# Recurrence of a two-block model on one core: v centred while it is turned, and the departing unit's steps moved

## The reference, cut to what matters

```python
def step(state, inp):
    r_t, w_t, k_t, v_t, aa_t, bb_t = inp
    sa = jnp.einsum('bhij,bhj->bhi', state, aa_t)
    state = (state * w_t[:, :, None, :] + sa[..., None] * bb_t[:, :, None, :]
             + v_t[..., None] * k_t[:, :, None, :])
    y = jnp.einsum('bhij,bhj->bhi', state, r_t)
    return state, y
...
mu = jnp.mean(y, axis=-1, keepdims=True)
var = jnp.mean(jnp.square(y - mu), axis=-1, keepdims=True)
yn = (y - mu) * lax.rsqrt(var + GN_EPS)
yn = yn * gn_w + gn_b
bonus = jnp.sum(r_h * k_h * r_k.astype(jnp.float32), axis=-1, keepdims=True) * v_h
out = (yn + bonus) * heads(g)
```

## Time and profile before

| | us |
|---|---|
| runs before the change | 3271.34, 3264.36, 3263.5 |
| median | 3264.36 |
| profiled execution, its own time | 3259.7 |
| its span in the profile | 3257.9 |
| TensorE busy (matmuls) | 3078.1 |
| VectorE busy | 1979.6 |
| ScalarE busy | 1417.1 |
| mean granted TensorE clock | 0.984 of full speed |

### The profile page before, as it was taken

The page is one execution under the profiler, slowest core; times in us unless marked ns, Lnnn a source line. Parts: engine busy times, 40 slices in busy tenths (PEclk is TensorE's granted clock), DMA queues, the critical chain, the costliest instruction groups (busy, mean ns, idle before and its releaser), DMA issues.

```text
span 3257.9 us, 46321 instructions
## 1 busy us (share of the span) xinstructions
PE 3078.1 (94%) x18478; PEld 2345.0 (72%) x18478; DVE 1979.6 (61%) x3370; ACT 1417.1 (43%) x2611; POOL 0.2 (0%) x4
## 2 busy tenths in 40 slices
PE   8988999999999999899999999888899999999888
PEld 7446666688888887778888666666646887787766
DVE  3635667667666656875555476666543666656675
ACT  2313555645333334553334455555412554444343
POOL 0000000000000000000000000000000000000000
PEclk9999999999999999999999899999999999999999
DMA  7510000042333356543333400000043334455545
GB/s 272 194 46 1 1 1 1 13 155 68 94 104 97 104 173 220 178 153 98 118 109 107 164 17 18 22 20 17 19 157 137 126 106 144 142 184 203 185 164 181
DMA packets 254519, 351.27 MB, mean 108 GB/s; under 512 B 12384, under 2 KB 142048, under 8 KB 251104
## 3 DMA queue, kind: packets, MB, share of 16 engines
q1 hardware_dynamic: 254304, 348.30, 32.0%
HBM read 263.84 MB, written 84.41 MB: 107 GB/s over the span
## 4 chain that ended last, share of the span: by engine, by line
PE 73%; DVE 11%; DMA 8%; issue 4%; ACT 3%; SPq 0%; DVEq 0%; ACTq 0%
PE ps L198 71%; DMA wr<-in_w_down 6%; DVE wl L406 3%; DMA hid<-ob 2%; PE ps L1572 1%; DVE NM L2429 1%; PE ps L934 1%; ACT wh L382 1%; PE ps L2868 0%; DMA wr<-hid 0%; DVE MM L3187 0%; DVE ob L1325 0%; DVE Yf L507 0%; DVE QT L2448 0%; DVE RT L2447 0%
## 5 line engine op out<-in xcount | busy, mean ns | idle before, releaser
L198 PE MATMUL ps<-ffn_h,wh 128*128 128x512 f32 x2176 | 672.9, 390 | 12.4 <-DVE ob L1325 9.2
L406 DVE TENSOR_TENSOR wl<-wr,wh 128x512 fp32r<-128x512 f32 x610 | 403.2, 688 | 276.0 <-ACT wh L382 272.5
L382 ACT ACTIVATE wh<-wr 128x512 fp32r<-128x512 f32 x610 | 363.9, 624 | 459.7 <-PE ps L198 280.4
L198 PEld LDWEIGHTS ps<-ffn_h,wh 128*128 128x128 f32 x2176 | 408.0, 188 | 101.7 <-DVE ob L1325 13.5
L198 PE MATMUL ps<-ffn_h,wl 128*128 128x512 f32 x1088 | 423.9, 390 | 0.0
L198 PE MATMUL ps<-in_h,wh 128*128 128x512 f32 x1200 | 371.0, 390 | 4.5 <-DVE Yf L836 4.5
L198 PE MATMUL ps<-wh,wh 128*128 128x512 f32 x756 | 301.5, 399 | 46.1 <-DVE wl L406 46.0
L198 PE MATMUL ps<-wl,wh 128*128 128x512 f32 x756 | 298.3, 395 | 0.0
L198 PE MATMUL ps<-wh,wl 128*128 128x512 f32 x756 | 298.1, 394 | 0.0
L198 PEld LDWEIGHTS ps<-in_h,wh 128*128 128x128 f32 x1200 | 225.8, 188 | 52.2 <-DVE Yf L836 4.9
L198 PEld LDWEIGHTS ps<-ffn_h,wl 128*128 128x128 f32 x1088 | 204.6, 188 | 42.9
(11 more groups left out here) (370 smaller groups left out, 5126.1 us busy)
## 6 DMA issues: line engine op xcount, KB each, us to landing
hid<-ob SPq DMA_DIRECT2D x174, 256.0 KB, 2.3
wr<-hid SPq DMA_DIRECT2D x84, 512.0 KB, 4.4
wr<-in_w_down SPq DMA_DIRECT2D x72, 512.0 KB, 3.7
wr<-in_w_up SPq DMA_DIRECT2D x54, 512.0 KB, 4.3
wr<-in_w_in SPq DMA_DIRECT2D x42, 512.0 KB, 5.1
kept<-ob SPq DMA_DIRECT2D x84, 256.0 KB, 2.0
late<-in_w_ada SPq DMA_DIRECT2D x16, 1024.0 KB, 7.2
wr<-in_w_out SPq DMA_DIRECT2D x32, 512.0 KB, 4.2
```

Source lines behind the costliest of these rows:

```text
L198: return e.op.matmul(out, left, right, start=start, stop=stop, skip_group_check=True)
L382: e.op.activation(self.rows(s)[0], src, ACT.Copy).then_inc(*e.event(self.name + "_act", ("w_high", self.name, s)))
L406: e.op.tensor_tensor(lo, src, hi.bitcast(F32), ALU.subtract).then_inc(*e.event(self.name + "_dve", ("w_low", self.name, s), *done))
```

## The change

- v's rows are no longer made by four transposes but by four float32 products of v's blocks with a new 128x128 constant, `centre` (identity minus 1/64 within each head), so they come out with the head's mean removed. The constants grow by 128 columns.
- The mean product, and VectorE's subtraction of the mean, go. VectorE's addition after yt writes into the other tile of the pair.
- Leaving, in steps: ScalarE's Square goes from 12 to 11, Ln and Exp from 14 to 16, VectorE's multiplication from 15 to 17, gate_mm from 16 to 17, affine from 16 to 18, bonus from 17 to 19, VectorE's last product from 18 to 20.
- Entering, in steps: b's rows on TensorE go from 19 to 16, their copy from 19 to 17; k's rows from 20 to 18, their copy from 20 to 19; VectorE's L2996, which makes k's input, from 19 to 16.
- On ScalarE the entering unit's instructions now stand ahead of the leaving unit's within a step.

```diff
--- before.py
+++ after.py
@@ -26,7 +26,7 @@
 CONSTS = {}
 _at = 0
 for _name, _n in [("ident", 128), ("ones", 128), ("bones", 128), ("dc", 128), ("ds", 128), ("mA16", 64),
-                  ("mAoff", 64), ("mNR", 128), ("mKR", 128), ("id64", 64), ("eps", 4)]:
+                  ("mAoff", 64), ("mNR", 128), ("mKR", 128), ("centre", 128), ("id64", 64), ("eps", 4)]:
     CONSTS[_name] = (_at, _n)
     _at += _n
 NCONST = _at
@@ -54,6 +54,7 @@
     put("mAoff", ~same & (col < row))
     put("mNR", np.concatenate([same & (row < col), row <= col], 1))
     put("mKR", np.concatenate([row < col, row <= col], 1))
+    put("centre", (r == q) - (r // 64 == q // 64) / 64.0)
     put("id64", (r % 64) == np.arange(64)[None, :])
     o, _ = CONSTS["eps"]
     c[:, o] = EPS
@@ -2847,16 +2848,22 @@
         self.sums_tensor(e, ("bonus", j), 6, E2[:, :], ("rk", j))
         for _ in range(3):
             yield
-        self.rows_tensor(e, j, "v_rows", lambda i: v[:, i * 128:(i + 1) * 128], ("shifted", "v", j))
+        group = ("v_rows", j)
+        _, free = k.settle(group, 6)
+        e.wait_ge(free, ("shifted", "v", j))
+        for i in range(4):
+            x = mm(e, k.out(group, 128, 128 * i), v[:, i * 128:(i + 1) * 128], k.cst("centre"), True, True)
+        x.then_inc(*e.event("mix_mm", ("mm", group)))
         yield
         yield
         c = 8 * (j % 2)
         self.rows_tensor(e, j, "a_rows", lambda i: self.AR[:, 0, c + 2 * i:c + 2 * i + 2, :].rearrange("p a n -> p (a n)"), ("at", j))
-        for _ in range(4):
-            yield
+        yield
         self.rows_tensor(e, j, "b_rows", lambda i: a_[:, i * 128:(i + 1) * 128], ("b_end", j))
         yield
+        yield
         self.rows_tensor(e, j, "k_rows", lambda i: k_[:, i * 128:(i + 1) * 128], ("k_end", j))
+        yield
         yield
 
     def rows_tensor(self, e, j, what, src, ready):
@@ -3275,10 +3279,10 @@
                 x = mm(e, k.out(group, 64, c % 8 * 64, slice(part, part + 64)), self.STt[part:part + 64, c, :], self.R2[part:part + 64, c * 64:(c + 1) * 64], True, True)
         x.then_inc(*e.event("mix_mm", ("mm", group)))
         yield
-        self.sums_tensor(e, ("mean", j), 7, Yt[:, :], ("read", ("yt", j)))
         yield
         yield
         self.sums_tensor(e, ("var", j), 7, Yt[:, :], ("centred_sq", j))
+        yield
         yield
         yield
         yield
@@ -3293,12 +3297,12 @@
     def leave_scalar(self, e, j):
         k, hp = self.k, j // 2
         Yt, yc = self.GN
-        for _ in range(12):
+        for _ in range(11):
             yield
-        e.wait_ge(("read", ("mean", j)), ("mm", ("mean", j)))
+        e.wait_ge(("read", ("yt", j)))
         e.op.activation(Yt[:, :], yc[:, :], ACT.Square).then_inc(*e.event("mix_act", ("centred_sq", j)))
-        yield
-        yield
+        for _ in range(5):
+            yield
         e.wait_ge(("mm", ("var", j)))
         e.op.activation(Yt[:, :], k.out(("var", j)), ACT.Ln, scale=1.0 / 64, bias=k.eps(1)).then_inc(*e.event("mix_act", ("read", ("var", j))))
         e.wait_ge(("read", ("var", j)))
@@ -3326,15 +3330,15 @@
                     *e.event("chunk_dve", ("state", j, c + 1), ("read", group)))
             yield
         e.wait_ge(("mm", ("yt", j)))
-        e.op.tensor_tensor(Yt[:, :], k.out(("yt", j)), self.Y0[:, sl], ALU.add).then_inc(*e.event("mix_dve", ("read", ("yt", j))))
-        yield
-        e.wait_ge(("mm", ("mean", j)), ("read", ("yt", j)))
-        e.op.scalar_tensor_tensor(yc[:, :], k.out(("mean", j)), -1.0 / 64, Yt[:, :], ALU.mult, ALU.add).then_inc(*e.event("mix_dve", ("read", ("mean", j))))
-        yield
-        yield
-        yield
-        yield
-        e.wait_ge(("group_rstd", j), ("read", ("mean", j)))
+        e.op.tensor_tensor(yc[:, :], k.out(("yt", j)), self.Y0[:, sl], ALU.add).then_inc(*e.event("mix_dve", ("read", ("yt", j))))
+        yield
+        yield
+        yield
+        yield
+        yield
+        yield
+        yield
+        e.wait_ge(("group_rstd", j), ("read", ("yt", j)))
         e.op.tensor_tensor(yc[:, :], yc[:, :], Yt[:, :], ALU.mult).then_inc(*e.event("mix_dve", ("normed", j)))
         yield
         yield
@@ -3401,7 +3405,7 @@
         for j in range(self.UNITS):
             behind = [self.leave_scalar(e, j - 1)] if j else []
             ahead = [self.enter_scalar(e, j + 1)] if j + 1 < self.UNITS else []
-            together(*behind, *ahead, self.chunk_scalar(e, j))
+            together(*ahead, *behind, self.chunk_scalar(e, j))
         e.mark(("end", "chunks", e.name))
         together(self.leave_scalar(e, self.UNITS - 1), self.gates.first_scalar(e))
```

More of the change, by code:

```diff
@@ L2925, in enter_scalar @@
         yield
+        self.rows_copy(e, j, "b_rows", self.Btm)
         yield
         yield
-        self.rows_copy(e, j, "b_rows", self.Btm)
+        self.rows_copy(e, j, "k_rows", self.Ktm)
         yield
-        self.rows_copy(e, j, "k_rows", self.Ktm)
         yield
```

## The result

| | before | after |
|---|---|---|
| median, us | 3267.85 (3263.5 to 3279.54, 4 runs) | 3325.4 (3318.8 to 3349.95, 4 runs) |
| profiled execution, us | 3259.7 | 3323.86 |
| its span, us | 3257.9 | 3322.1 |
| mean granted TensorE clock | 0.984 | 0.954 |

The ratio is 1.0184, with a 95% interval of 1.0125 to 1.0243: the change costs about 60 us, and 3231 us was forecast. The kernel before itself takes about 3,380 us in some executions (7 of its 42 in the comparisons of this study), which the ratios leave out.

A forecast was written before the change was run, and what follows sets the result against it. TensorE, busy 94% of the span, was taken as the bound, with waits between engines in the recurrence. Terms summed to 33 us saved, 3259.7 to 3226.7 profiled; 4.7 added for the median gave 3231 us, range 3222 to 3240 (chance 0.57).

The forecast's parts named there:

- Unit 0 enters beside attention: +0.5 if nothing hides it.: Attention, where unit 0 enters ahead of the recurrence: a cost of 0.5 us if nothing hides it.
- b's rows, 1.1 us: Middle chunks, before y1: TensorE idles 1.1 us until ScalarE's copy of a's rows frees bank 6.
- 27.0 + 4.6 + 1.1 + 0.1: Recurrence savings in us: chunks 1 to 5 27.0, chunk 6 4.6, chunk 7 1.1, chunk 0 0.1.
- 0.3 us from holding y2's additions: Middle chunks, step 17: VectorE's multiplication ends at 2132.4, y2's additions can start at 2132.7, so no cost.
- 5.4 us per chunk: Chunks 1 to 5: the next chunk's a starts at 2140.3 instead of 2145.64, 5.4 us sooner per chunk.
- the new wait before rate: Chunk end: rate waits for VectorE's last product of the leaving unit to free bank 7, starting at 2139.75 instead of 2138.8.
- v's product against transposes: Chunk, v's rows: four float32 products take 1.16 us against 0.58 for four transposes, +0.58 us.
- Rival B: 3240 to 3249 us: time returns in new waits, a late Exp before y2's additions or v's products at 2.3 us; chance 0.20.
- E: Slower, 3275 us or more: VectorE's multiplication in step 17 holds y2's additions, out, state and the next chunk; chance 0.03.
- D: About 3262 us: copy of v's rows still late, TensorE still idle over 3 us, clock still falling; chance 0.05.
- C: 3214 to 3222 us: the added waits before b's rows and before rate are covered by TensorE's remaining work; chance 0.15.
- The last unit's mean product: Behind the recurrence, where the last unit leaves beside full TensorE work: dropping its mean product saves 0.9 us.

The follow-up runs named there:

- experiment 4: Kernel before, with unit 0's v turned by four float32 products with the identity instead of four transposes: 3263.52 us (one run).
- experiment 1: Changed kernel, but unit 0 turns b's and k's rows in the old steps: 3232.37 us, ratio 0.9888.
- experiment 2: Kernel before, with only unit 0's b's and k's rows (products, copies, L2996) in the new, earlier steps: 3357.93 us, ratio 1.0292.
- experiment 3: Changed kernel, with unit 0's b's rows in PSUM bank 7 instead of 6: 3249.23 us; repeated 3229.64, 3229.9, 3234.19 and 3357.83 us.
- experiment 6: Kernel before, with unit 0's copy of a's rows and its b's rows both in step 17: 3390.48 us; repeated 3359.17 us, ratio 1.0277.
- experiment 8: On experiment 1, rate one step later for units 1 to 7: 3237.69 us; then also b's rows, gate_mm and all behind it later: 3240.37 us.
- experiment 7: Experiment 1 with one part taken back: Ln and Exp block 3249.32 us; v's transposes and mean product 3239.22; b's and k's rows 3231.05, repeated 3245.55.

## Why the prediction was wrong

- **The step that failed** is "Unit 0 enters beside attention: +0.5 if nothing hides it." It costed v's product alone, and for that it was right: 0.99 us to the next start against 0.53 for the transposes at that place, +0.46 (experiment 4). But the change also moves b's rows, k's rows and L2996 of unit 0, and these were never walked through the attention. Walked, they show it: the copy of a's rows stands behind the attention's exponentials on ScalarE, and b's rows had been moved into that copy's step. The wait is 1.87 us and the clock costs the rest: +91.5 us (experiments 1, 2, 3, 6). The forecast made just this walk for the eight chunks and found the same kind of wait there (b's rows, 1.1 us); it didn't repeat it for the one unit whose neighbours are other work.
- **The clock** was read in the earlier trace rows as a price of a 3.16 us stand, to be gained back. That a new, shorter stand could lower it elsewhere was not asked. The trace of before would have allowed the question, though not its size. In its chunks the clock falls after the 3.16 us and is back some 3.4 us later (2129.9 to 2133.3 in chunk 2). At the start of its attention it falls beside a stand of 1.81 us and stays low for 20 us (1857 to 1877):

```profile
1857.09 1.09 PE L1572 MATMUL ps<-CN,P 128*128 128x128 f32 x4 [1.81 <-ACT PT L1608]
```

  Nothing in it suggested 190 us.
- **The recurrence, step by step.** From 335.5 to 303.1 us: -32.4 where the forecast's terms for it give 27.0 + 4.6 + 1.1 + 0.1 = 32.8. In the middle chunks, from the start of a: v's rows 1.25 us sooner (forecast 1.31); a's rows 3.97 sooner (3.9 for g2); y1 4.99 sooner (5.0); the wait before b's rows 0.97 (1.1). VectorE's multiplication was 0.3 us from holding y2's additions by the forecast; it starts at 2226.17, lasts 0.69, and the additions, for which it leaves VectorE 0.16 us of idle time, follow at 2227.02: it costs nothing, as forecast.
- **A term mis-sized:** 5.4 us per chunk. Five chunks went from 44.35 us (2057.44 to 2279.20) to 39.38 (2155.26 to 2352.16): 4.97. The price of the new wait before rate is the main part of what is missing. The wait stands at the end of all five chunks. In chunks 1, 3 and 5 rate starts 1.51 to 1.56 us after decay; in chunks 2 and 4 decay itself waits 0.40 us for the copy of k's rows, and rate starts 1.09 us after it, which the merged row hides and the row of its weights shows:

```profile
2232.06 2.21 PE L199 MATMUL ps<-TH,WA 64*128 64x512 f32 x4 [0.40 <-ACT F L2890]
2233.15 0.29 PEld L199 LDWEIGHTS ps<-TH,WA 64*128 64x128 f32 x2 [0.79 <-DVE ybT L3349]
```

  The forecast took half of the pair's 1.06 us for each product, 1.5 us from decay to rate and 0.55 from rate to a. But before, decay and rate (64 rows each) run side by side: both are done in 1.06 us (four records in 1.13 us). Alone, rate takes as long as the pair: two records in 1.12 us, 1.05 to a. So decay to a takes 2.41 us on average instead of 1.06, a loss of 1.35 where 1.0 was forecast.
- **What differs from chunk to chunk** is something else, which no term has: in chunks 1, 3 and 5 TensorE stands for 0.84 to 1.25 us in the middle of state, and the profile shows no engine that it waited for:

```profile
2192.95 0.28 PE L199 MATMUL ps<-F,MM 64*64 64x64 f32 x4 [1.25 <-issue]
```

  These chunks last 39.8 to 40.8 us, the two without it 38.1 (a's starts at 2155.26, 2196.06, 2234.20, 2273.96, 2312.11 and 2352.16). The kernel before has such a stand in each of the five, of 0.16 to 1.16 us. What makes it isn't known.
- **Luck in the sum.** The five chunks gave 24.9 us against 27.0 forecast, the rest of the recurrence 7.6 against 5.8: chunk 6 gained 6.6 (4.6 forecast), chunk 7 1.7 (1.1), and chunk 0 lost 0.7 (0.1 gained). The total is right to 0.4 us because these errors cancel.
- **v's product against transposes.** Before, four transposes took 0.58 us to the next start; after, the four products, eight records, take 1.09 in chunk 2 (2215.62 to 2216.71): +0.51, forecast +0.58. The Trainium skill, "TensorE: Matmul & The Clock Gate", section Terms, has the transpose mode as four times faster for FP32. Against products of the same shape the traces don't bear that out: 1.09 to 0.58 us in the chunk, 0.99 to 0.53 in the attention, both 1.9 times. Rival B's dearer product falls with it.
- **What each part was worth** was left unsaid in the forecast. The leaving unit's logarithm carries 20 us, the centring 3 to 7 in the recurrence, the sooner b and k nothing that was seen.
- **The rivals.** E named the right side with the wrong place: VectorE in step 17, which cost nothing. Its chance of 0.03 was the chance of that one mishap, not of any slower outcome. D fell: the low clock in the chunks is gone in the kernel after (experiment 1's trace, the same there, still has it at two places). B and C fell for the kernel as a whole; C's mechanism is real only when more steps are moved (experiment 8: 39.4 to 38.1 us per chunk).

The last unit's mean product, 0.9 forecast, lies in the rest, which is 0.6 us shorter; that is too little to tell from no change.

Open: why the clock stays low so long in the attention, while TensorE is full; what besides the length of a stand makes it fall; stands between 0.81 and 1.87 us, which weren't tried there; and what decides, from one execution to the next, how long the low stretch at the attention's start lasts.

## What to carry to other kernels

A step that is moved in a shared helper is moved for every caller: walk each kind of neighbour it gets, the one exceptional unit first, and ask of each engine's queue what now stands ahead of the copy that frees its buffer. A stand of the full engine is priced twice, by its length and by the clock that it may cost; where the stage behind it stays at the low level, as this attention does, 2 us become 90. And when a gain is bundled from several edits, price each alone: here the one that brought nothing carried the loss.

## What the hardware showed beyond that

- A stand of 1.87 to 2.00 us in the attention was followed by 190 to 200 us at the 1.2 GHz level with TensorE busy for practically all of it (187.10 of 188 us, 180.00 of 180, 160.00 of 160). The recurrence, with TensorE busy for 235.23 of 265 us, ran at 1.00 throughout.
- In all five traces in which the low level held so long (the kernel after, experiments 2 and 6, the fourth execution of experiment 3), it ended at the same place in the program: in the attention's last group, 32 transposes in a row (2110.76 in the kernel after), 2.6 to 5.0 us after that group began. Why there isn't shown.
- The attention of every kernel starts with some microseconds of low clock, also the one before (0.50 over 1860 to 1870). It is over after 20 to 27 us mostly, after 44 to 58 in others, or not before the attention's last group. That makes most of the spread between equal kernels; 3,358 us in experiment 3 and 3,390 in experiment 6 were of this kind.
- How long that first stretch lasts goes with what follows the stand of 1.81 us, which 14 of the 16 traces have there. TensorE's next stand, for VectorE's scaling of the attention's output O, is 0.47 to 1.05 us in the nine of them with a short stretch and 1.40 to 2.11 in the five with one of 44 us or more. No experiment sets it, so which is the cause isn't shown. In the other two traces (experiment 2, and the single run in experiment 7 with b's and k's rows back) the clock fell sooner, about 1 us behind a stand of 0.34, and was low for 27 us.
- The same stands can be followed by a fall in one execution and not in another: the recurrence of experiment 1's trace falls to 0.50 at about 2103 and 2182, behind stands of 0.84 to 1.24 and 0.41 to 0.44 us, which the kernel after has too, at 1.00.
